# Two of four weight-block sums of each D_FF tile by accumulating DMA, in a ring of seven weight slots

## What is computed

```python
for layer in range(DEPTH):          # 2
    h = h + 0.5 * swiglu(rms_norm(h, norm_ffn1[layer]), ffn1_w_gate[layer], ffn1_w_up[layer], ffn1_w_down[layer])
    hn = rms_norm(h, norm_mix[layer])
    h = h + (even_mixer(hn, ...) if layer % 2 == 0 else fourier_mixer(hn, w_out_fourier[0]))
    h = h + 0.5 * swiglu(rms_norm(h, norm_ffn2[layer]), ffn2_w_gate[layer], ffn2_w_up[layer], ffn2_w_down[layer])
return rms_norm(h, norm_final)[:, N_META:]
# swiglu(x, g, u, d) = (silu(x @ g) * (x @ u)) @ d
```

## Time and profile before

| | us |
|---|---|
| median of three runs | 2608.82 (2608.74 to 2614.94) |
| the profiled execution | 2607.15 |
| its span, first to last instruction | 2605.3 |
| TensorE busy in the span | 2496.2 (96%) |
| VectorE busy | 1657.6 (64%) |
| ScalarE busy | 1046.5 (40%) |
| GpSimd busy | 90.9 (3%) |
| mean granted TensorE clock | 0.978 of full |

### The profile page before, as it was taken

The page is one execution under the profiler, slowest core; times in us unless marked ns, Lnnn a source line. Parts: engine busy times, 40 slices in busy tenths (PEclk is TensorE's granted clock), DMA queues, the critical chain, the costliest instruction groups (busy, mean ns, idle before and its releaser), DMA issues.

```text
span 2605.3 us, 35440 instructions
## 1 busy us (share of the span) xinstructions
PE 2496.2 (96%) x13644; PEld 2415.1 (93%) x13644; DVE 1657.6 (64%) x2900; ACT 1046.5 (40%) x2015; POOL 90.9 (3%) x101
## 2 busy tenths in 40 slices
PE   4999999999999899999999999999999699999997
PEld 4999999999449899999999999999998699999996
DVE  7756665752544757574677656665754875767574
ACT  6433343431553534243455433343443542434241
POOL 0000000014000000000000000000002200000000
PEclk9999999999889999999999999999999799999998
DMA  2212111121001111211111112111121112212121
GB/s 101 73 65 73 65 66 64 69 95 60 17 1 49 49 57 65 73 65 65 65 65 55 68 65 73 65 65 65 69 75 37 67 53 70 72 66 81 65 69 63
DMA packets 28247, 166.29 MB, mean 64 GB/s; under 512 B 3376, under 2 KB 3632, under 8 KB 15536
## 3 DMA queue, kind: packets, MB, share of 16 engines
q1 hardware_dynamic: 26496, 160.64, 17.7%
q10 hardware_dynamic: 1584, 3.38, 0.3%
HBM read 160.73 MB, written 3.28 MB: 63 GB/s over the span
## 4 chain that ended last, share of the span: by engine, by line
PE 71%; issue 22%; DVE 4%; ACT 2%; POOL 1%; DMA 0%; POOLq 0%; ACTq 0%; DVEq 0%
PE banks L1361 26%; PE banks L1438 13%; PE banks L1440 13%; PE banks L1439 13%; PE banks L1491 2%; PE banks L1526 1%; PE banks L1505 1%; PE banks L1354 1%; DVE xf_lo L972 1%; ACT xf L615 0%; DVE xf_lo L985 0%; POOL w_sum L516 0%; POOL w_sum L518 0%; PE banks L1400 0%; ACT xf_hi L626 0%
## 5 line engine op out<-in xcount | busy, mean ns | idle before, releaser
L1438 PE MATMUL banks<-xf_hi,w_hi 128*128 128x400 f32 (+2 forms) x2464 | 848.7, 344 | 70.3 <-DVE xf_lo L985 23.4
L1439 PE MATMUL banks<-xf_lo,w_hi 128*128 128x400 f32 (+2 forms) x2464 | 848.7, 344 | 0.0
L1440 PE MATMUL banks<-xf_hi,w_lo 128*128 128x400 f32 (+2 forms) x2464 | 846.1, 343 | 0.0
L1438 PEld LDWEIGHTS banks<-xf_hi,w_hi 128*128 128x128 f32 x2464 | 466.3, 189 | 73.6 <-issue 51.7
L1440 PEld LDWEIGHTS banks<-xf_hi,w_lo 128*128 128x128 f32 x2464 | 468.5, 190 | 0.0
L1439 PEld LDWEIGHTS banks<-xf_lo,w_hi 128*128 128x128 f32 x2464 | 466.7, 189 | 0.4
L566 ACT ACTIVATE w_hi<-raw 128x512 fp32r<-128x512 f32 (+3 forms) x564 | 310.4, 559 | 373.5 <-PE banks L1361 365.6
L1361 PE MATMUL banks<-act_hi,w_lo 128*128 128x400 f32 (+2 forms) x1408 | 366.4, 341 | 0.0
L1361 PE MATMUL banks<-act_lo,w_hi 128*128 128x400 f32 (+2 forms) x1408 | 366.2, 341 | 0.0
L1361 PE MATMUL banks<-act_hi,w_hi 128*128 128x400 f32 (+2 forms) x1408 | 365.7, 341 | 0.0
L566 ACT ACTIVATE w_hi<-w_sum 128x512 fp32r<-128x512 f32 x368 | 230.3, 630 | 332.7 <-DVE w_sum L895 128.6
(11 more groups left out here) (162 smaller groups left out, 2453.1 us busy)
## 6 DMA issues: line engine op xcount, KB each, us to landing
raw<-gate_up_dram SPq DMA_DIRECT2D x88, 1024.0 KB, 4.8
raw<-down_dram SPq DMA_DIRECT2D x32, 768.0 KB, 4.2
raw<-down_dram SPq DMA_DIRECT2D x32, 640.0 KB, 3.9
raw<-w_in_dram SPq DMA_DIRECT2D x5, 1024.0 KB, 4.8
raw<-w_fourier_dram SPq DMA_DIRECT2D x8, 576.0 KB, 3.8
raw<-w_out_dram SPq DMA_DIRECT2D x4, 1024.0 KB, 4.8
h<-x_dram ACTq DMA_DIRECT2D x8, 400.0 KB, 9.0
y_dram<-h SPq DMA_DIRECT2D x8, 400.0 KB, 2.5
```

What stands on the lines that cost most here:

```text
L1438: M.matmul(out, a_hi, b_hi, start=fresh and k == 0, stop=False, skip_group_check=True)
L1439: M.matmul(out, a_hi, b_lo, start=False, stop=False, skip_group_check=True)
L1440: ins = M.matmul(out, a_lo, b_hi, start=False, stop=k == KP - 1, skip_group_check=True)
```

## The change

A21 no longer comes with the raw load, which has three quarters (768 KB). For S1 and S3 SyncE loads A21 straight into the unit's `w_sum` slot (`first_block`), once `unit_done` frees it, and GpSimd then issues a DMA that adds A22 (for S1) or A11 (for S3) in place (`add_block`, `pair_sums`). ScalarE's `w_hi` of those units waits for that DMA, as does VectorE's sum S2. VectorE keeps S2 = S1 + A11 and S4 = S2 + A12. The ring has seven slots, `SUM_AHEAD` is 4. As an accumulating DMA adds only, the order and signs of blocks change on the host (the up weights' A11 and A12 parts, the forms T1, T2, N4 and the factor -0.5 where the down result is added to h). The projections' weights are loaded by 512 KB. GpSimd's additions are put between its other work, in order.

```diff
-QUARTER_AT = {"A11": 0, "A21": QUARTER, "A12": 2 * QUARTER, "A22": 3 * QUARTER}
-NS = 6
-SUM_AHEAD, HI_AHEAD, LO_AHEAD = 5, 4, 3
-RAW_COLS = 4 * QUARTER
+QUARTER_AT = {"A11": 0, "A12": QUARTER, "A22": 2 * QUARTER}
+A21_AT = 3 * QUARTER
+NS = 7
+SUM_AHEAD, HI_AHEAD, LO_AHEAD = 4, 4, 3
+RAW_COLS = 3 * QUARTER
...
-            W_UNITS.append(Unit("raw", len(LOADS), (r % 2) * 2 * QUARTER + half * QUARTER, QUARTER))
-        if r % 2:
-            LOADS.append(((name, r // 2), RAW_COLS))
-            LAST_UNIT[len(LOADS) - 1] = len(W_UNITS) - 1
+            W_UNITS.append(Unit("raw", len(LOADS), half * QUARTER, QUARTER))
+        LOADS.append(((name, r), 2 * QUARTER))
+        LAST_UNIT[len(LOADS) - 1] = len(W_UNITS) - 1
...
+        def first_block(n):
+
+            u = W_UNITS[n]
+            _, f, j = LOADS[u.load][0]
+            if n >= NS:
+                sp.wait_ge(unit_done, n - NS + 1)
+            sp.dma_start(w_sum[:, n % NS, :], gate_up[f, j, :, A21_AT:A21_AT + QUARTER])\
+                .then_inc(a21_in[u.kind], 16)
+
+        waiting = sorted(DMA_SUM_AT)
...
+                    while waiting and waiting[0] - NS < LAST_UNIT[before] - LO_AHEAD:
+                        first_block(waiting.pop(0))
                     sp.wait_ge(w_ready, LAST_UNIT[before] + 1)
...
+        def add_block(f, j, kind):
+
+            n = GU[f][j] + WEIGHT_OF.index(kind)
+            at = QUARTER_AT["A22" if kind == "S1" else "A11"]
+            pool.wait_ge(a21_in[kind], DMA_SUM_AT[n])
+            pool.dma_start(w_sum[:, n % NS, :], gate_up[f, j, :, at:at + QUARTER], accum_op=ALU.add)\
+                .then_inc(a_added[kind], 16)
+
+        def pair_sums(f, first, last):
+            for j in range(first, last):
+                add_block(f, j, "S1")
+                add_block(f, j, "S3")
+
+        pair_sums(0, 0, 1)
         power(norm_of("ffn1_0"))
+        pair_sums(0, 1, FF_TILES)
...
+            if m == KD - 1:
+                add_block(3, 0, "S1")
             pool.wait_ge(odd_done, m + 1)
...
+        add_block(3, 0, "S3")
         power(norm_of("ffn2_1"))
+        pair_sums(3, 1, FF_TILES)
...
+            elif u.kind in ("S1", "S3"):
+                act.wait_ge(a_added[u.kind], DMA_SUM_AT[n])
+                source = w_sum[:, n % NS, 0:u.cols]
...
-            if u.kind == "S1":
-                ins = V.tensor_tensor(out, quarter(u, "A21"), quarter(u, "A22"), ALU.add)
-            elif u.kind == "S2":
+            if u.kind == "S2":
+                dve.wait_ge(a_added["S1"], DMA_SUM_AT[n - 1])
+                ins = V.tensor_tensor(out, w_sum[:, (n - 1) % NS, :], quarter(u, "A11"), ALU.add)
+            else:
                 dve.wait_ge(sum_made, SUM_AT[n - 1])
-                ins = V.tensor_tensor(out, w_sum[:, (n - 1) % NS, :], quarter(u, "A11"), ALU.subtract)
-            elif u.kind == "S4":
-                dve.wait_ge(sum_made, SUM_AT[n - 1])
-                ins = V.tensor_tensor(out, quarter(u, "A12"), w_sum[:, (n - 1) % NS, :], ALU.subtract)
-            else:
-                ins = V.tensor_tensor(out, quarter(u, "A11"), quarter(u, "A21"), ALU.subtract)
+                ins = V.tensor_tensor(out, w_sum[:, (n - 1) % NS, :], quarter(u, "A12"), ALU.add)
...
-                ins = V.tensor_tensor(form(f, "T2", k), form(f, "B22", k), form(f, "T1", k), ALU.subtract)
+                ins = V.scalar_tensor_tensor(form(f, "T2", k), form(f, "T1", k), -1.0, form(f, "B22", k),
+                                             ALU.mult, ALU.subtract)
```

More of the change, by code:

```diff
@@ L153 @@
 N_LOADS = len(LOADS)
-SUM_AT, FOLD_AT = {}, {}
+SUM_AT, DMA_SUM_AT, FOLD_AT = {}, {}, {}
 for _n, _u in enumerate(W_UNITS):
-    if _u.kind[0] == "S":
+    if _u.kind in ("S1", "S3"):
+        DMA_SUM_AT[_n] = 16 * (len(DMA_SUM_AT) // 2 + 1)
+    elif _u.kind[0] == "S":
         SUM_AT[_n] = len(SUM_AT) + 1
@@ L283, in build @@
     raw_full = [sem(f"raw_full{s}") for s in range(2)]
+    a21_in = {"S1": sem("s1_a21_in"), "S3": sem("s3_a21_in")}
+    a_added = {"S1": sem("s1_added"), "S3": sem("s3_added")}
     sum_made = sem("sum_made")
@@ L355, in source @@
             if what[0] == "gate_up":
-                return gate_up[what[1], what[2]]
+                return gate_up[what[1], what[2], :, 0:RAW_COLS]
             if what[0] == "down":
@@ L367, in _ @@
                 else:
+                    while waiting and waiting[0] - NS < LAST_UNIT[before] - LO_AHEAD:
+                        first_block(waiting.pop(0))
                     sp.wait_ge(w_ready, LAST_UNIT[before] + 1)
             sp.dma_start(raw[n % 2][:, 0:cols], source(what)).then_inc(raw_full[n % 2], 16)
-            if what == ("w_in", 2):
+            if what == ("w_in", 4):
                 sp.wait_ge(unit_done, WIN[0])
@@ L374, in _ @@
                                  dst[:].rearrange("p a b c d -> p (a b c d)"), src[:, :]).then_inc(mix_in, 16)
+        for n in waiting:
+            first_block(n)
         for k in range(KD):
@@ L498, in _ @@
             pool.wait_ge(pooled_done, g + 1)
+        pair_sums(1, 0, 1)
         power(norm_of("ffn2_0"))
+        pair_sums(1, 1, FF_TILES)
+        pair_sums(2, 0, 1)
         power(norm_of("ffn1_1"))
+        pair_sums(2, 1, FF_TILES)
         pool.wait_ge(unit_done, WF[0])
@@ L917, in first_sums @@
             for n in range(SUM_AHEAD - LO_AHEAD):
-                if W_UNITS[n].kind[0] == "S":
+                if W_UNITS[n].kind in ("S2", "S4"):
                     weight_sum(n)
@@ L955, in form_sum @@
                 dve.wait_ge(gained, f * KD + 2 * k + 1)
-                ins = V.tensor_tensor(form(f, "T1", k), b12[:, 0:C], form(f, "B11", k), ALU.subtract)
+                ins = V.tensor_tensor(form(f, "T1", k), form(f, "B11", k), b12[:, 0:C], ALU.subtract)
             elif name == "T2":
@@ L964, in form_sum @@
                 dve.wait_ge(form_added, ADD_AT[f, "T2", k])
-                ins = V.tensor_tensor(form(f, "N4", k), form(f, "B21", k), form(f, "T2", k), ALU.subtract)
+                ins = V.scalar_tensor_tensor(form(f, "N4", k), form(f, "T2", k), -1.0, form(f, "B21", k),
+                                             ALU.mult, ALU.subtract)
             ins.then_inc(form_added, 1)
@@ L979, in late_forms @@
             dve.wait_ge(form_added, ADD_AT[f, "T3", KP - 1])
-            V.tensor_tensor(xf32[:, FORM_AT["N4"], :, 0:C], xf32[:, FORM_AT["B21"], :, 0:C],
-                            xf32[:, FORM_AT["T2"], :, 0:C], ALU.subtract).then_inc(form_added, 1)
+            V.scalar_tensor_tensor(xf32[:, FORM_AT["N4"], :, 0:C], xf32[:, FORM_AT["T2"], :, 0:C], -1.0,
+                                   xf32[:, FORM_AT["B21"], :, 0:C], ALU.mult, ALU.subtract)\
+                .then_inc(form_added, 1)
             dve.wait_ge(form_added, ADD_AT[f, "N4", 0])
@@ L1047, in add_to_h @@
             if len(FFN_TOKENS[f][1]) == 1:
-                return V.scalar_tensor_tensor(two(h[:, m, :]), slot(2 + m % 2), 0.5, two(h[:, m, :]),
+                return V.scalar_tensor_tensor(two(h[:, m, :]), slot(2 + m % 2), -0.5, two(h[:, m, :]),
                                               ALU.mult, ALU.add)
@@ L1727 @@
             u = columns(a[f"ffn{f}_w_up"][layer], KD).reshape(FF_TILES, P, KD, P)
-            gate_up.append(np.concatenate([g[:, :, 0::2], u[:, :, 0::2], g[:, :, 1::2], u[:, :, 1::2]], axis=2)
-                           .reshape(FF_TILES, P, RAW_COLS))
+            gate_up.append(np.concatenate([g[:, :, 0::2], g[:, :, 1::2], u[:, :, 1::2], u[:, :, 0::2]], axis=2)
+                           .reshape(FF_TILES, P, 4 * QUARTER))
             for half in range(2):
@@ L1753 @@
         "tables": dft_tables(), "gate_up": np.stack(gate_up), "down5": np.stack(down[0]),
-        "down6": np.stack(down[1]), "w_in": pairs(w_in), "w_out": pairs(w_out), "w_fourier": w_fourier,
+        "down6": np.stack(down[1]), "w_in": w_in, "w_out": w_out, "w_fourier": w_fourier,
     }
```

4 lines of the change are left out of this document (2 added, 2 removed).

## The result

The changed kernel takes **2736.41 us** (median of four runs, 2734.39 to 2743.64) for 2608.78 of the kernel before on the same chip: a ratio of 1.0488, 95% interval 1.0470 to 1.0507. The prediction was 2625 with a range to 2685. The direction was right, the size too small by a factor of eight. The profiled execution has a span of 2741.8 us for 2605.3: **136.5 us** are to be explained.

The account below looks back on a forecast made before the run. TensorE, busy in 96% of the span, was taken to bound the kernel, so work off VectorE pays only where TensorE waits for it. Terms -0.6 + 9.9 + 2.7 + 4.5 = +16.5 us gave 2625 us, range 2606 to 2685.

Parts of the forecast that it names:

- (c): Rival: FFN heads gain more than forecast and the late wait at the start is hidden, -4 to -9, 2602 us; chance 0.07.
- The window's length: In each tile, from slot free to the latest landing: 7.6 us; 7.4 in the first FFN, 7.2 in the last.
- Step 1: Sums S1 and S3 leave VectorE: 0 in full stretches, -0.6 us at the head of the third FFN.
- Step 2: Two transfers in a tile's window: S1 hidden at 7.0 us, S3 at 7.55 late in first and last FFN, +9.9 us.
- X: Time of GpSimd's accumulating second transfer: 4.35 us, from 2.65 plain, 0.7 reading the destination, 1.0 making descriptors.
- The first transfer: SyncE's A21 of 256 KB into the slot: 2.65 us for S1; S3 lands 3.2 us after its slot is free.
- Step 3: At the start, sums made one unit later (SUM_AHEAD 5 to 4) delay ScalarE's w_hi and TensorE: +2.7 us.
- Step 4: Before the last FFN, GpSimd's additions wait behind its work on h: +4.5 us, (X - 1.05) + (X - 3.1) in general.
- (a): Rival: accumulating DMA as quick as a plain one, X 2.65 to 4, no tile stalls, +4 to +6, 2614 us; chance 0.34.
- (b): Rival: GpSimd's issue held up beside a full VectorE, X = 5.05, tiles stall, +66, 2675 us; chance 0.23 with beyond.

Follow-up runs that it names:

- e4: Changed kernel without GpSimd's second transfers; ScalarE and VectorE wait for A21 alone, A22 and A11 left out: 2608.65 us, ratio 0.9982.
- e11: Changed kernel with w_hi 3, w_lo 2 and sums 4 units ahead, and A21 of S3 issued before the raw load: 2605.40 us, ratio 0.9990.
- e6: Changed kernel with each raw gate/up load of a tile after the first two cut from 768 KB to 8 KB: 2681.26 us, ratio 1.0278.
- e2: Changed kernel with GpSimd's second transfer as a plain copy overwriting the slot, without adding: 2657.57 us, ratio 1.0178.
- e3: Changed kernel with A21 of S3 issued ahead of the raw load on SyncE, not behind it: 2702.79 us, ratio 1.0351.
- e8: Changed kernel with only S1 made by GpSimd's adding transfer; VectorE adds S3 in its slot: 2656.39 us, ratio 1.0182.
- e9: Changed kernel with only S3 made by GpSimd's adding transfer; VectorE adds S1 in its slot: 2694.24 us, ratio 1.0327.
- e7: Kernel e1 (VectorE's additions in the slot, no GpSimd transfer) with SUM_AHEAD 5 instead of 4: 2601.00 us, ratio 0.9963.
- e1: Changed kernel with VectorE adding A22 or A11 to A21 in the slot, in place of GpSimd's accumulating DMA: 2612.22 us, ratio 1.0005.

## Why the prediction was wrong

**What bounds the kernel.** Right: work off VectorE is worth next to nothing (e4, e11), and the loss came where I looked for it, in the chain between a free slot and ScalarE's next duty. That nothing but VectorE's sums could gain was not right: the seventh slot gained too, see (c). The window's length was right. In the tile above the four units are 8.76 us and the chain overran its window by as much as TensorE stood: 9.62 - 7.6 = 2.02 = 10.78 - 8.76.

**Step 1** (sums off VectorE, -0.6): too small to be told apart; the whole third head gained 2.3.

**Step 2** (+9.9, measured +134) is the step that failed. Of its three terms the first held, and the other two did not.

1. *The adding transfer X*: predicted 4.35, measured 4.2 to landing and 4.21 to 4.28 to `w_hi`. Right, and with luck: of its parts 2.65 + 0.7 + 1.0, the adding measured 0.8, but a plain 256 KB takes 3.1 on SyncE's queue (e6) and only 0.3 more from GpSimd (3.4, e2), so that two errors met. The Trainium skill (DMA: Bandwidth & Descriptors, section Anatomy of one DMA — SWDGE (gpsimd) path) gives 2.0 us plus bytes/436 GB/s, an estimate of 2.6 us for such a transfer; the trace has 3.4 plain and 4.2 adding, and that decides.
2. *The first transfer*: predicted 2.65 for S1 and 3.2 for S3, measured 3.37 and 4.18 (means 3.58 and 4.38) to GpSimd's issue. This is the mis-sized term. A21 landed after 3.1 and 3.9 us (medians); the other 0.28 passes in nearly every pair between the landing and GpSimd's issue, and my sum had nothing for it. For the landing I took the 4.7 of one load of 1 MB and subtracted 2.05 for three quarters of its data, and did not use the other sizes on the same page of before:

```profile
raw<-gate_up_dram SPq DMA_DIRECT2D x88, 1024.0 KB, 4.8
...
raw<-w_fourier_dram SPq DMA_DIRECT2D x8, 576.0 KB, 3.8
```

From 1024 to 576 KB the landing falls by 1.0 us; at that rate 256 KB would land after 3.1 (an estimate). The same queue does take 3.1 us for 256 KB alone and 2.5 for 8 KB (e6), and the load of 768 KB lies close to one or the other A21 in every tile. In such a stretch A21 is late whether it is issued first or second (e3). With 3.37 for 2.65 the 7.0 of S1 becomes 7.7, already over the window; with 4.18 for 3.2 the 7.55 of S3 becomes 8.5.
3. *How often, and which value*: the forecast took one value for all pairs, and let a stall be paid once a tile. Pairs scatter (S1 median 7.78, mean 8.06), a wait counts when late and gives nothing when early, and both sums have their own window (e8 and e9 add up). With the measured means and 18 tiles an FFN, S3 alone is 72 x (8.60 - 7.6) + 18 x 0.2 + 18 x 0.4 = 83 us, for 80.1 in the trace. The prediction put 7 us on each 0.1 us in this chain. From the changed kernel to e2 both pairs shrink by 0.8 to 0.9 us and the tiles by 79 us, about 9 us for each 0.1 us (an estimate), and the chain was 0.8 to 0.85 longer than I took it.

Not in the working at all were the 32.8 us that TensorE's busy time grew, at the waits and in places of lower granted clock.

**Step 3** (start, +2.7): measured +3.8 at TensorE's first long run, +4.8 at the first copy of g. The mechanism was the one described, ScalarE waiting for sums that are now made a unit later:

```profile
28.98 0.63 ACT L614 ACTIVATE w_hi<-w_sum 128x512 fp32r<-128x512 f32 x1 [3.01 <-DVE w_sum L936]
...
39.49 0.63 ACT L614 ACTIVATE w_hi<-w_sum 128x512 fp32r<-128x512 f32 x1 [2.86 <-DVE w_sum L939]
```

The waits of 3.01 and 2.86 us fall on S2 and S4 as forecast (the earlier trace rows had the first `w_hi` at 25.52). With `SUM_AHEAD` 5 the start is at +1.4 (e7).

**Step 4** (before the last FFN, +4.5): right in mechanism, smaller in net. ScalarE and GpSimd after:

```profile
2153.46 0.63 ACT L614 ACTIVATE w_hi<-w_sum 128x512 fp32r<-128x512 f32 x1 [5.50 <-DMA w_sum<-gate_up_dram]
...
2148.24 1.07 POOL L584 TENSOR_TENSOR h<-h,odd 128x263 f32<-128x263 f32 x1
2149.25 0.93 POOL L490 DMA_DIRECT2D w_sum<-gate_up_dram  x1
```

S1's addition is issued behind GpSimd's work on h, and `w_hi` waits 5.50 us. TensorE's wait there rose from 15.45 to 19.41. From the first product of the Fourier projection to TensorE's start it is 71.56 us for 69.24, +2.3; without GpSimd's transfers (e4) it is 68.05, so that they cost 3.5 and something else in the change, not separated, gives 1.2 back. The forecast +4.5 was taken without the latter.

**Rivals.** (a), X from 2.65 to 4, fell with X; e2 shows moreover that even X = 3.4 loses 55 us in the tiles, where the working of (a) had none. (Its +2.1 for the last head at X = 2.65 is at most 1.6 by step 4's own formula, which decides nothing.) (b) forecast the larger time by GpSimd held up beside VectorE, X = 5.05: the time went its way, past it, and the mechanism is not there, with X at 4.2 to 4.3 and GpSimd's issues at 0.86 us (median; the longest is 1.05) beside a VectorE busy 57% of the span. The Trainium skill (SBUF — State Buffer, section Who interferes with whom) infers that tensor_tensor, nine tenths of VectorE's busy time here, does not hold up GpSimd's descriptor writing; the trace agrees.

(c), faster heads: the heads of the third and fourth FFN gained 2.3 and 2.5 us, those of the first two lost 4.8 and 2.6. In the second and fourth head there is a gain that neither (c) nor my working names, that of the seventh slot. Before the change ScalarE's `w_hi` waits in the fourth head until TensorE frees one of six slots, so the forms and the copy of g behind it in ScalarE's order are late, and TensorE stands a second time, until 0.09 us after that copy:

```profile
2065.93 0.63 ACT L566 ACTIVATE w_hi<-raw 128x512 fp32r<-128x512 f32 x1 [3.83 <-PE banks L1440]
...
2072.53 0.66 PE L1438 MATMUL banks<-xf_hi,w_hi 128*128 128x384 f32 x1 [3.25 <-issue]
```

The second head has the same two waits, 3.69 and 3.42 us. After the change they are gone, and with seven slots that `w_hi` starts at once:

```profile
2169.51 0.61 ACT L614 ACTIVATE w_hi<-raw 128x512 fp32r<-128x512 f32 x1
```

From TensorE's start to the first copy of g it is 5.85 us for 9.79 in the fourth head and 6.64 for 10.42 in the second; e1, e4 and e7, which have seven slots too, show 5.84 to 5.86 in the fourth. So the slot brings about 3.9 us in each, against 1.4 and 6.4 us lost ahead of TensorE's start.

**The range** failed because the one term that I held to be known, a transfer of 256 KB worked out from one of 1 MB, got no bounds, while its partner X had 2.65 to 8.5, and because S1's window was counted as hidden beside S3's.

**What stays open.** How the 32.8 us of TensorE's busy time split between clock and matmuls at a wait was only estimated, and what gives e7 2.0 us ahead of TensorE's start in the fourth FFN was not separated. The seventh slot was not run by itself: its gain is read from the waits of kernels that have it and of the one that has not. It was not tried whether a second queue for A21, in place of SyncE's, would let the change keep its deeper look-ahead.

## What to carry to other kernels

Before two dependent DMAs are put in place of an engine's instruction, count from the event that frees the buffer to the next duty of the in-order engine that takes the result, and compare with the mean of both landings, size by size, and with what shares their queue. A transfer's fixed part (2.5 us of the 3.1 to 3.3 here) is not divided by making it smaller, and from a landing to the next engine's issue another 0.28 us pass. If the chain does not fit, consuming one unit later gives it a whole unit (with the order of two transfers, all of the 134 us here) at a small price at the heads, while relieving an engine that nobody waits for gives nothing.

## What the runs showed of the hardware

- A DMA of 8 KB on SyncE's queue lands in 2.5 us, of 256 KB in 3.1 (both e6), of 768 KB in 4.2 (e1, e4), of 1 MB in 4.8 (median of 88, before): the data's part is small up to a quarter MB.
- An accumulating DMA of 256 KB by GpSimd lands in 4.2 us for 3.4 of a plain one. Of the 0.8, 0.33 are GpSimd's issue (0.87 for 0.54), the rest the transfer.
- From the landing of A21 to GpSimd's issue of the transfer that waits for it 0.28 us passed, in nearly all of the 176 pairs.
- Two transfers close together on one queue lengthen each other whichever went first: 256 KB landed in 3.9 us and took 4.2 to its consumer both ways (3.1 and 3.4 with the load cut to 8 KB), and the load of 768 KB went from 4.7 to 5.5 when it was issued second.
- In a stretch of 10 us in which TensorE stood 3.0 us the mean granted clock was 0.66 (24 matmuls), in the next, without a wait, 1.00 (57); before the change four such stretches in the tiles of the third FFN (1550 to 1570 and 1700 to 1720) had 1.00.
